# A transformer layer's first projections: fp32 over all tokens, or three fp32r passes over two halves of them

## The reference

```python
h = rmsnorm(x, norm1_w) * (1 + sc1) + sh1          # scale and shift from silu(c) @ w_mod
hc = rmsnorm(ctx, norm1_w) * (1 + csc1) + csh1
qa, ka, va, za, ... = split(h @ w_in)              # q, k, v, z: 4 heads of 128 channels each
# gdn_prep, for the latent tokens and for the context tokens apart:
qkv = silu(short_conv(concatenate([q, k, v])))     # 5 taps over tokens, per channel
q, k = l2norm(q), l2norm(k)                        # over the 128 channels of a head
q, k = axial_rope(q), axial_rope(k)                # latent tokens only
q = q * 128 ** -0.5
```

## Time and profile before

| what | value |
|---|---|
| median of three runs | 3834.86 us |
| profiled execution, whole | 3836.23 us |
| its span in the profile | 3834.7 us |
| PE busy, share of the span | 3657.0 us, 95% |
| DVE | 2320.1 us, 61% |
| ACT | 1638.0 us, 43% |
| POOL | 855.4 us, 22% |
| mean granted TensorE clock | 0.977 of full speed |

### The profile page before, as it was taken

One profiled execution on the slowest core, in us unless ns is written; L12 is line 12 of the kernel. 1 busy time (PEld: TensorE's weight loads), 2 busy tenths in 40 slices (PEclk: granted clock), 3 DMA queues, 4 the chain that ended last, 5 costly groups with the idle time before them and its releaser, 6 DMA issues. The chain is left out here.

```text
span 3834.7 us, 58126 instructions
## 1 busy us (share of the span) xinstructions
PE 3657.0 (95%) x19520; PEld 2934.2 (77%) x19520; DVE 2320.1 (61%) x3546; ACT 1638.0 (43%) x3000; POOL 855.4 (22%) x812
## 2 busy tenths in 40 slices
PE   8999999999997999989999999896799999999998
PEld 3444459976767999968787788785688888888887
DVE  4655632555656999943434353444767777677775
ACT  4333333335654666642424242322344444444442
POOL 3888400011106666610000000000000010000100
PEclk9999999999998999999999999997899999999999
DMA  7455455131115334243434342443467676776763
GB/s 284 153 139 143 123 183 131 59 83 42 25 45 190 119 119 124 91 178 118 165 104 168 100 167 77 146 154 135 138 214 225 216 220 205 213 225 214 219 210 91
DMA packets 258770, 570.98 MB, mean 149 GB/s; under 512 B 38972, under 2 KB 117340, under 8 KB 256348
## 3 DMA queue, kind: packets, MB, share of 16 engines
q1 hardware_dynamic: 225612, 451.18, 37.0%
q0 software_dynamic: 33040, 118.25, 10.4%
HBM read 458.27 MB, written 100.73 MB: 146 GB/s over the span
## 5 line engine op out<-in xcount | busy, mean ns | idle before, releaser
L3034 DVE TENSOR_TENSOR sb_we_low<-sb_we,sb_we_high 128x1024 fp32r<-128x1024 f32 x384 | 466.5, 1223 | 121.5 <-ACT sb_we_high L2985 121.5
L2985 ACT ACTIVATE sb_we_high<-sb_we 128x1024 fp32r<-128x1024 f32 x377 | 392.2, 1048 | 142.3 <-PE ey L2949 142.3
L2396 DVE TENSOR_TENSOR sb_wm_low<-sb_wm,sb_wm_high 128x1024 fp32r<-128x1024 f32 x127 | 155.4, 1224 | 402.0 <-ACT sb_wm_high L2309 402.0
L336 PE MATMUL p_ps<-sb_hT,sb_ring 128*128 128x512 f32 (+1 forms) x960 | 373.2, 549 | 0.0
L336 PEld LDWEIGHTS p_ps<-sb_hT,sb_ring 128*128 128x128 f32 x960 | 181.9, 190 | 186.2 <-issue 181.3
L2250 PE MATMUL pg<-sb_hb_high,sb_wm_high 128*128 128x512 f32 x768 | 303.8, 396 | 9.5 <-DVEq L2368 5.4
L2252 PE MATMUL pg<-sb_hb_high,sb_wm_low 128*128 128x512 f32 x768 | 300.5, 391 | 0.0
L2251 PE MATMUL pg<-sb_hb_low,sb_wm_high 128*128 128x512 f32 x768 | 300.4, 391 | 0.0
L2932 PE MATMUL eg<-sb_xe_parts,sb_we_high 128*128 128x512 f32 x1024 | 260.5, 396 | 1.6 <-DVE sb_xe_parts L3029 1.6
L2932 PE MATMUL eu<-sb_xe_parts,sb_we_high 128*128 128x512 f32 x1024 | 259.1, 395 | 0.0
L2894 POOL DMA_INDIRECT out<-sb_ybe,sb_ti x32 | 51.0, 1595 | 880.5 <-DVE sb_ybe L3069 822.5
(11 more groups left out here) (409 smaller groups left out, 8656.9 us busy)
## 6 DMA issues: line engine op xcount, KB each, us to landing
sb_we<-in_w_ex SPq DMA_DIRECT2D x384, 512.0 KB, 4.4
sb_wm<-in_w_gates SPq DMA_DIRECT2D x96, 512.0 KB, 3.6
sb_stage<-in_w_mod_row POOLq DMA_DIRECT2D x64, 256.0 KB, 3.7
sb_stage<-h_d SPq DMA_DIRECT2D x32, 512.0 KB, 4.7
sb_wm<-in_w_br SPq DMA_DIRECT2D x32, 512.0 KB
sb_ring<-in_w_ch POOLq DMA_DIRECT2D x19, 512.0 KB, 5.2
sb_gr<-gc_d SPq DMA_DIRECT2D x36, 256.0 KB, 3.8
sb_lk<-k_d SPq DMA_DIRECT2D x36, 256.0 KB, 4.0
```

The lines of the kernel that those rows point to most:

```text
L336: last = nc.tensor.matmul(ps[:, b % BANKS, 0:wd], w[:, kind, k], hT[:, k, t0:t0 + wd], start=(k == 0), stop=(k == KD - 1))
L2396: v.tensor_tensor(wl[n], w[n], wh[n], ALU.subtract).then_inc(s.wl, 1)
L2985: nc.scalar.activation(wh[:, n % CUT], w[:, n % RAW], ACT.Copy).then_inc(s.wh, 1)
L3034: v.tensor_tensor(wl[:, n % CUT], w[:, n % RAW], wh[:, n % CUT], ALU.subtract).then_inc(s.wl, 1)
```

## The change

In `delta_inputs` the 2304 tokens are cut into two halves of 1152, with a margin of two tokens for the convolution. Each half has its own 12 tiles of 1154 columns (three blocks each) and two gate tiles, so 28 tiles where there were 14. The rows of a half are normalised in one of three landing buffers, split into high and low parts (`hx`) and stay on chip for the half; the second half's rows are squared, summed, normalised and modulated between windows 3 and 13 of the first, one third of them is read again from `h_d`, and they are split when the halves change (window 14). Each weight is split too (`wx`, two buffers): `high_weight(p + 1)` and `low_weight(p + 1)` stand first in window p on ScalarE and VectorE. There is no register loop any more. Swaps are four DMAs instead of eight; stores are two or three per tensor and half. The row parts run on GpSimd in windows 3 to 23, about three for each weight load.

Elsewhere: a `Scope` clears all semaphores of a stage at once (17 clearings become 10; at the end of `mixer` 2 in place of 6); the first position in `delta_rule` waits for its gate row, for keys and queries, and for their transposes separately, and loads them in that order; `merge` moves its roots ahead of the gate's sigmoid and splits two weights of `project_out` in its last tile.

```diff
+class Scope(ExitStack):
+    def __init__(self, nc):
+        super().__init__()
+        self.nc, self.made = nc, []
+        self.callback(self.clear)
+    def clear(self):
+        self.nc.clear_and_free_semaphores(self.made)
+        self.nc.all_engine_barrier()
...
+    OWN = T // 2
+    FROM = [0, OWN - PAD]
+    CUTS = [[(0, CTX), (CTX, 450), (CTX + 450, 448)], [(0, 386), (386, 384), (770, 384)]]
+    GATES = [[(CTX, 448), (CTX + 448, 448)], [(PAD, 384), (PAD + 384, 384), (PAD + 768, 384)]]
...
                 for k in range(KD):
-                        last = nc.tensor.matmul(ps[:, b % BANKS, 0:wd], w[:, kind, k], hT[:, k, t0:t0 + wd],
-                                                start=(k == 0), stop=(k == KD - 1))
+                        high, low = (wx[:, p % 2, part, k * P:(k + 1) * P] for part in range(2))
+                        rh, rl = (hx[:, part, k, off:off + wd] for part in range(2))
+                        nc.tensor.matmul(bank, high, rh, start=(k == 0), stop=False)
+                        nc.tensor.matmul(bank, high, rl, start=False, stop=False)
+                        last = nc.tensor.matmul(bank, low, rh, start=False, stop=(k == KD - 1))
...
+                def load_weight(p):
+                    half, h, kind = TILES[p]
+                    wait(pool, s.wl, p - 2)
+                    pool.dma_start(w[:, p % 3], g.w_ch[3 * H + kind if h is None else kind * H + h]).then_inc(s_w[p % 3], 16)
...
+                def high_weight(p):
+                    act.wait_ge(s_w[p % 3], 16 * (p // 3 + 1))
+                    if p >= 2:
+                        act.wait_ge(s.proj, ENDS[p - 2])
+                    a(wx[:, p % 2, 0], w[:, p % 3].rearrange("p k c -> p (k c)"), ACT.Copy).then_inc(s.wh, 1)
...
+                for p in range(NP):
+                    one, two = stage(p - 1), stage(p - 2)
+                    nb = len(BLKS[p])
+                    if p == NP // 2:
+                        high_rows(NBK)
+                        high_rows(NBK + 1)
+                    if 0 < p < NP - 1:
+                        high_weight(p + 1)
+                    if p == NP // 2:
+                        evict(p, 0)
+                        high_rows(NBK + 2)
+                    else:
+                        evict(p, 0)
                     if one:
-                        activate(*one)
-                    if new:
-                        copy_raw(*new, range(BANKS, NB))
+                        activate(*one[0:3])
+                    for b in range(1, nb):
+                        evict(p, b)
                     if one and one[1] < 2:
-                        logs(*one)
+                        logs(*one[0:2])
                     if two and two[1] > 0:
-                        copy_turned(*two)
+                        copy_turned(*two[0:2])
                     if one and one[1] < 2:
-                        reciprocal_roots(*one)
+                        reciprocal_roots(*one[0:2])
+                    if p in (3, 6, 10):
+                        squares(NBK + (3, 6, 10).index(p), (0, 1))
+                    if p in (4, 7, 11):
+                        squares(NBK + (4, 7, 11).index(p), (2, 3))
+                    if p in (5, 8, 12):
+                        inverse_root(NBK + (5, 8, 12).index(p))
+                    if p in (8, 11, 13):
+                        modulate(NBK + (8, 11, 13).index(p))
...
+                for p in range(NP):
+                    one, two = stage(p - 1), stage(p - 2)
                     two = two if two and two[1] < 2 else None
+                    if p == NP // 2:
+                        low_rows(NBK)
+                        low_rows(NBK + 1)
+                    if 0 < p < NP - 1:
+                        low_weight(p + 1)
+                    if p == NP // 2:
+                        low_rows(NBK + 2)
                     if one:
                         convolve(*one, (0, 1))
                     if two:
-                        norm(*two)
+                        norm(*two[0:2])
                     if one:
                         convolve(*one, (2, 3, 4))
                     if two:
-                        rotate(*two)
+                        rotate(*two[0:3])
+                    if p in (7, 10, 13):
+                        normalise(NBK + (7, 10, 13).index(p))
...
@@ delta_rule
-                for u in range(2):
-                    for d in range(2):
-                        load(d, pos(d, u), u)
+                for d in range(2):
+                    sp.dma_start(gr[d][0][:], g.gc_d[d, pos(d, 0)].partition_broadcast(P)).then_inc(s[d].lg, 16)
+                for d in range(2):
+                    sp.dma_start(lk[d][0][:], g.k_d[pos(d, 0)]).then_inc(s[d].lk, 16)
+                    sp.dma_start(lq[d][0][:], g.q_d[pos(d, 0)]).then_inc(s[d].lk, 16)
...
@@ merge
                         for br in range(NBR):
+                            if near == 0 and br > 0:
+                                root(b + 1, (2 * br - 2, 2 * br - 1))
                             act.wait_ge(s.gate, NBR * m + br + 1)
                             act.wait_ge(s.prod, used(m, br))
                             a(sg[:, br], pg[br][:], ACT.Sigmoid).then_inc(s.sig, 1)
...
-                            if near == 0 and br > 0:
-                                root(b + 1, (2 * br - 2, 2 * br - 1))
```

More of the change, by code:

```diff
@@ L120, in sems @@
-    c.callback(clear)
+    c.made += list(made.values())
     return namedtuple("Semaphores", list(made))(**made)
 BANKS = 3
[L125 to L147, removed]
@@ L374, in mod_columns @@
                     last.then_inc(s.colt, 1)
-                def norm_sums(b):
-                    wd = BLOCKS[b][1]
-                    wait(pe, s.nln, b - 1)
-                    for j in range(2):
-                        pe.wait_ge(s.nadd, 2 * b + j + 1)
-                        for i in range(2):
-                            last = nc.tensor.matmul(pn[:, b % 2, 0:wd], g.ones, sqr[:, j, i, 0:wd],
-                                                    start=(j == 0 and i == 0), stop=(j == 1 and i == 1))
-                        last.then_inc(s.nsumh, 1)
@@ L424, in window @@
                     if one and one[1] < 2:
-                        sums(*one)
+                        sums(*one[0:2])
                     if two and two[1] > 0:
-                        transpose(*two)
-                windows(nc.tensor, window)
+                        transpose(*two[0:2])
             @block.scalar
             def _(act):
-                act.sem_inc(s.rawp, NB)
-                act.wait_ge(s.cld, 16)
-                nc.scalar.activation(cs[:], cc[:], ACT.Silu).then_inc(s.sc, 1)
@@ L451, in modulate, with squares @@
-                def modulate(b):
-                    t0, wd = BLOCKS[b]
-                    which = 1 if b == 0 else 0
+                a = nc.scalar.activation
+                def squares(i, js):
+                    buf = NORMS[i][2]
+                    wd = SPLITS[NORMS[i][1]][1]
+                    if i == 5:
+                        act.wait_ge(s.x4, 16)
+                    else:
+                        act.wait_ge(s_x[buf], 16 * loads(i))
+                    for j in js:
+                        wait(act, s.nsumh, 4 * i + j - 1 if i >= NBK else 4 * (i - 1) + j + 1)
+                        a(squared(i, j), landing(buf, wd)[:, 2 * j:2 * j + 2], ACT.Square).then_inc(s.nsq, 1)
@@ L479, in activate @@
                     own = Steps(act, s.silu, 2 * t)
[L480 to L481 removed]
+                    own.done(a(sl[:, kind, 0:CTX], cv[:, 0:CTX], ACT.Silu))
+                    skip = 0 if half else PAD
+                    own.done(a(sl[:, kind, CTX:OWN], cv[:, CTX + skip:OWN + skip], ACT.Silu))
                     if kind < 2:
@@ new lines, in _ @@
+                normalise(0)
+                low_weight(0)
+                low_rows(0)
+                normalise(1)
+                low_rows(1)
+                normalise(2)
+                low_rows(2)
+                low_weight(1)
+                dve.wait_ge(s.cvw, 16)
+                for p in range(NP):
+                    one, two = stage(p - 1), stage(p - 2)
+                    two = two if two and two[1] < 2 else None
+                    if p == NP // 2:
[5 more added lines that the diff above has]
+                        low_rows(NBK + 2)
```

707 lines of the change are left out of this document (405 added, 302 removed).

## The result

The changed kernel takes 3916.97 us (median of 4, 3912.04 to 3917.45), the kernel before 3837.26 in the same sitting: a ratio of 1.0209, with an interval of 1.0194 to 1.0224. It is 80 us slower. The forecast was 3876, 41 us slower, with 3915 as its upper bound: the sign was right, the size was not.

A forecast was written before the change was run, and what follows sets the result against it. The ring through ScalarE, VectorE and TensorE replaces TensorE as the first stage's bound, 59 us later; the other edits give 18 back: 3834.9 + 59 - 18 = 3876 us. Range 3790 to 3915, the forecast itself 3848 to 3900.

The forecast's parts named there:

- The ring: First stage: a loop through ScalarE, VectorE and TensorE, one turn per half tile, sets the pace; 20.3 us with k.
- Rival (1): First stage: TensorE stays the bound and the kernel gets faster, 3773 us; chance 0.14.
- Through the buffer `cv`: First stage: convolution, ScalarE's square and TensorE's sums share `cv`; each step waits for the one before through it and queue order.
- The window, 20.3, 19.0 and 17.6 to 18.7: First stage, time per half tile: 20.3 us for k, 19.0 for q, 17.6 (second half 18.7) for v.
- GpSimd's row parts at nothing: First stage: GpSimd needs 16.6 us a window, 19 with added squares, under the ring's pace, so costed at nothing.
- The stage's timeline: First stage, summed window by window from TensorE's start near 57: ends at 610 us against 551, 59 us later.
- Change of halves: First stage, between halves: last eviction, copies, modulate and splitting hold TensorE 9.5 us; the third block's reload takes 7 us.
- rival (3): First stage: TensorE's pauses lower its clock, 18 us on top in q windows, 3894 us; chance 0.15.
- Rival (2): First stage: GpSimd's pace bounds, weights late behind row parts, 21 windows of 17.2 us, 3793 us; chance 0.10.
- The table load, 1.30 us and no drain: First stage, ScalarE: next activation 1.30 us after the load began; the skill's drain would add 44 us, not counted.
- The other edits, 18 us: Rest of the kernel: delta rule start 5, merge 9, output projection 1.3, and clearings; together 18 us earlier (11 to 23).
- rival (4): Delta rule start: finer first waits bring nothing, loads share DMA engines; 3881 us; chance 0.60 jointly with the forecast.

The follow-up runs named there:

- opening the ring: Changed kernel with two convolution buffers in turn and the low weight part behind the five taps on VectorE: 3836.09 us, ratio 1.0002 to the kernel before.
- the order: Changed kernel with one edit, the low weight part behind the five taps on VectorE instead of ahead of them: 3844.54 us.
- Without row sums: Changed kernel with GpSimd's 56 scalings and 56 additions of row parts cut to four columns, loads and stores kept: 3871.21 us.
- the other edits alone: First stage as in the kernel before, everything else as in the changed kernel: 3822.12 us, ratio 0.9964 to the kernel before.
- the run with the scalings on ScalarE: Kernel with two buffers, low part behind taps and late transposes of k (3825.47 us), its 64 row scalings moved from GpSimd to ScalarE: 3848.64 us.
- the scalings alone: Changed kernel with GpSimd's 56 scalings of row parts whole and its 56 two-input additions left out: 3885.36 us.

## Why the prediction was right in kind and short in size

**The ring takes TensorE's place: right.** TensorE's gift is real: the last blocks of 384 columns follow each other after 4.2 us, 8 x 384 x 1.35 ns = 4.15. It goes to waste as forecast, since one pass in place of three changed nothing, and opening the ring gave 81 us. Rival (1), TensorE stays the bound, is excluded by the same two runs.

**Through the buffer `cv`: wrong name, right walk.** A second buffer gave 2 us, the order 72. The walk had exponential, high part, low part, taps in a row, and that is the binding loop; the sums, which free the buffer, are done before the exponential. Had I asked of each link "what if this one is cut", the walk itself would have shown it.

**The window, 20.3, 19.0 and 17.6 to 18.7: near on average, wrong in its terms.** Where GpSimd has no row parts any more, the last windows of v, q and k (23 to 25) take 20.8, 18.8 and 17.8 us, 57.5 together. The forecast for a head of the second half was 58.0, but 55.4 with the 6 us that it takes off for the last seven windows; that the sum comes so near is in part luck, with one window put too long and one too short. The k window is 2.5 shorter than forecast: its Silu starts 10.0 us behind the high part, not 12.3, because the last three taps begin 1.45 us apart, not 1.55, and the first table load lies in ScalarE's wait for them, not behind it. The v window is 2.1 longer: its last pair-swap lands 14.0 us behind the high part, not 11.7. Heads 1 and 2 took 66.1 and 66.6 us, some 5 of them for the normalising of the second half.

**"GpSimd's row parts at nothing": the step that failed.** I asked only whether GpSimd was late. The price sits in the earlier trace rows: the mean tap was 2.99 us, the shortest 2.61. I took the difference for a share of the length and halved it with the tap: the forecast has 1.55 us a tap, where the shortest half tap takes 1.41 and the mean is 1.72. It is a price per collision, and it does not halve. The norm, shortest, median and longest in ns, in the kernel before:

```profile
L609 DVE SCALAR_TENSOR_TENSOR sb_sl<-sb_rsb,sb_sl x8: 2546/2616/3621, 136.2 to 492.0; 128x2304 f32<-128x2304 f32 x8
```

and half as wide, in the changed kernel:

```profile
L731 DVE SCALAR_TENSOR_TENSOR sb_sl<-sb_rsb,sb_sl x16: 1351/2434/2453, 111.6 to 608.2; 128x1152 f32<-128x1152 f32 x16
```

The worst is 1.08 us over the shortest at full width and 1.10 at half width, and what was the exception is now the median. What the price is can be read from the starts. In the kernel before, an addition had begun ahead of four of the eight norms, and 0.25, 0.48, 1.20 and 1.20 us of it were left; these norms are 0.12, 0.35, 1.07 and 1.07 us longer than the rest. In the changed kernel it was nine of 16, with 1.22 to 1.24 us left and 1.08 to 1.10 longer; 16 taps with 1.1 left are 0.9 longer. So the step is longer by about what is left of the addition, and the addition did not get shorter when the step did. There are still 56 additions, now beside steps half as long that all lie on the path; in the kernel before VectorE had 152 us of idle before its first tap to lose them in the earlier trace rows. Without them the mixer starts at 608.0, against my 610 plus the 3.5 us from handover to first matmul, 613.5. Beyond that halved share the term was put at 0, less 6 for the windows without GpSimd; measured, the row sums are 42 us of stage time, 46 of the whole.

**The stage's timeline.** The step by step account of the other 37 us of miss in the traced stage (646.8 at the handover, forecast 610): window 3 starts at 128.2 (122), window 12 at 324.8 (308), window 15 at 390.7 (362), window 26 at 603.8 (569). Without row sums these are 119.0, 294.1, 359.5 and 561.6, each below the forecast. So the row sums are the cause of all of it, and the other terms together were put a little too high. One of them was too low: the forecast counts five pairs of squares in windows 3 to 11 where the code has six, 1.7 us more.

**Change of halves.** 9.5 us from the last gate to the next tile: 9.2 measured. The reload at 7, an estimate between two rows: 13.5 from issue to landing, 10 us of the run. The row of 14.9 us, 1024 KB, was the nearer one to a load of 1536 KB; I set it aside for its queueing, and should have gone by its size.

**End of the stage.** ScalarE waits 9.4 us from its last copy's end to the mixer's first step; forecast 6.5 + 1.8.

**The clock, rival (3).** TensorE was granted 0.89 in the stage against 1.00 before, so the mechanism is there. The rival puts it on top of the q windows. In the last of them (window 24) TensorE was granted 0.50 at first and took 5.98 us for its first block, against 4.47 in the window behind it at full clock; the window still took 18.8 us, no more than the 19.0 of the walk without a clock term. One window is shown so; no run sets the clock apart in the whole stage. Rival (2), weights late behind row parts: GpSimd waited 107.9 us for VectorE instead.

**The table load, 1.30 us and no drain.** In the trace above the eviction starts 1.29 us after the load (182.37, 183.66). The Trainium skill's rule (ScalarE: Activation LUTs, What ACT_TABLE_LOAD costs) would have added 44 us and given, by accident, a sum near the measured time; the trace does not agree with it here.

**The other edits, 18 us: measured 13.** Merge 9, measured 12.1. Output projection 1.3, measured 1.9. Clearings 2.65: 1.5 of them at the entry to the delta rule, and there they are, in the wait that the forecast took from the earlier trace rows, 3.8 us there and now:

```profile
DVE sb_bar L2239 <- PEq L122: 2.3, 1, 2.3
```

At the end of the first stage, where 0.75 were expected, nothing is to be seen: from TensorE's last matmul to ScalarE's first step of the mixer it is 2.47 us before and 2.49 with the other edits alone. From the last matmul of all to the end of the program it is 15.6 and 15.3, about the 0.4 expected. Delta rule 5: 35.3 us after the mixer's last matmul became 30.6 for the same product further on (1186.39 and 1279.81), 4.7 less, and 1.5 of that are the clearings, so 3.2 are left for the finer waits, of which 2.3 remain at the merge. TensorE's first product there comes only 1.3 us sooner (its wait for loads was 13.8 and is 12.5); rival (4), finer waits bring nothing, is right for that product and falls for what follows.

## What to carry to other kernels

This ring through several in-order engines was opened by moving the step that closes it, not by giving buffers to it: cut each link on paper and see which cut shortens the walk. Work on GpSimd is not free because nobody waits for it; where two-input steps of VectorE are on the path, count the additions that will have begun ahead of such a step, at up to the length of the addition each and not as a share of the step, and let VectorE do small additions itself if it has idle time.

## What the hardware showed

The collision of GpSimd and VectorE, in sizes. With a two-input addition of GpSimd begun ahead of it the norm goes from 1.35 to 2.45 us, and a rotation step beside one from 1.10 to 2.15. Where the norm begins first it keeps its 1.36 us and the addition takes 1.84, as in the run with the scalings on ScalarE. With the scalings alone all norms stay at 1.35, taps take 1.42 to 2.04, and the first tap, with one input, averages 937 ns, against 842 without row sums. GpSimd pays as well: its scalings, 1.73 us as a rule, took 4.90 and 4.54 where VectorE had begun its normalising (350.33) and splitting (361.32) just ahead of them:

```profile
350.38 4.90 POOL L344 TENSOR_SCALAR sb_stage<-sb_stage,sb_cs 128x512 f32<-128x512 f32 x1 [1.94 <-DMA sb_stage<-in_w_mod_row]
...
361.57 4.54 POOL L344 TENSOR_SCALAR sb_stage<-sb_stage,sb_cs 128x512 f32<-128x512 f32 x1
```

The Trainium skill (SBUF — State Buffer, Who interferes with whom) says that an instruction of VectorE with two SBUF inputs contends with an instruction of GpSimd that reads SBUF, and that the order of issue decides which of the two is held up. For additions the traces agree: all nine norms of the changed kernel with an addition begun ahead of them are 1.1 us longer, and the eight norms that began ahead of the addition, in the run with the scalings on ScalarE, are not. The page makes no difference between a scaling and an addition; here 80 us of additions cost 32 us and 119 us of scalings 14, and in the kernel before two norms that began while a scaling had been running for 2.2 and 1.4 us took the 2.55 us of the undisturbed ones. Why the scaling is so much cheaper is open.

The second thing is a bound on TensorE where another loop sets the pace: with a third of the passes and 0.69 of the clock in place of 0.89, 24 windows took 3 us more in 500. How that divides between less work and a slower clock was not measured.
